# Two fused transformer blocks on one core: the input comes back for the residual tile by tile, into other memory, and the rotary angles are computed later

## The reference

```python
h = rms_norm(x, norm_mix_g[l])
p = h @ w_in[l]
...                      # 8 heads: a chunkwise mLSTM (y_a) and stick-breaking attention (y_b)
y = gates[..., :D_MODEL] * y_a + gates[..., D_MODEL:] * y_b
x = x + y.astype(x.dtype) @ w_out[l]
h2 = rms_norm(x, norm_mlp_g[l])
x = x + jnp.square(jax.nn.relu(h2 @ w_up[l])) @ w_down[l]
```

## Time and profile before

| what | us |
|---|---|
| median of three runs | 1381.68 |
| the profiled execution, its own time | 1377.67 |
| span of that execution, first to last instruction | 1375.9 |
| PE busy | 1319.2 |
| DVE busy | 701.8 |
| ACT busy | 635.1 |
| POOL busy | 101.5 |

### The profile page before, as it was taken

How to read it: one execution, slowest core, us unless ns; L and a number is a source line. 1 busy time by engine, 2 the same in 40 slices (tenths; PEclk the granted TensorE clock), 3 DMA queues, 4 the chain that set the end, 5 groups by cost and what they waited for, 6 DMA issues and landing times.

```text
span 1375.9 us, 16463 instructions
## 1 busy us (share of the span) xinstructions
PE 1319.2 (96%) x5984; PEld 1057.5 (77%) x5984; DVE 701.8 (51%) x1176; ACT 635.1 (46%) x926; POOL 101.5 (7%) x215
## 2 busy tenths in 40 slices
PE   6999999999999997999999999999868999999999
PEld 5787877878777786788888888878656777777887
DVE  5445444544444453542443524453698888435671
ACT  5645455563556552431322313354725545545830
POOL 1000010100001010000000000000121111111000
PEclk9999999999999999999999999999987999999999
DMA  5322212122221224132222322243111233533611
GB/s 200 104 69 96 69 65 84 57 95 69 95 69 65 99 60 158 51 114 81 91 91 95 102 108 91 91 134 116 62 61 39 100 122 104 185 116 130 244 62 61
DMA packets 26531, 134.42 MB, mean 98 GB/s; under 512 B 3320, under 2 KB 4408, under 8 KB 13696
## 3 DMA queue, kind: packets, MB, share of 16 engines
q1 hardware_dynamic: 16992, 107.49, 22.4%
q0 software_dynamic: 4896, 17.03, 3.8%
q10 hardware_dynamic: 4608, 9.44, 1.8%
HBM read 121.35 MB, written 11.55 MB: 97 GB/s over the span
## 4 chain that ended last, share of the span: by engine, by line
PE 89%; DVE 5%; ACT 3%; DMA 2%; issue 1%; POOL 0%; DVEq 0%; ACTq 0%; POOLq 0%
PE proj L291 71%; PE pa L1331 2%; PE pm L1288 1%; DMA x_res<-in_x 1%; PE pm L1338 1%; PE pa L1295 1%; PE pm L1451 1%; PE pa L1451 1%; PE pa L1288 1%; PE pa L1433 1%; PE pm L1433 1%; PE pa L1308 1%; PE pm L1443 1%; DVE rope L1048 1%; PE pm L1317 1%
## 5 line engine op out<-in xcount | busy, mean ns | idle before, releaser
L291 PE MATMUL proj<-h_hi,w_hi 128*128 128x512 f32 x960 | 385.6, 402 | 2.6 <-ACT sq_q L551 1.7
L291 PE MATMUL proj<-h_hi,w_lo 128*128 128x512 f32 x960 | 375.0, 391 | 0.0
L291 PE MATMUL proj<-h_lo,w_hi 128*128 128x512 f32 x960 | 374.7, 390 | 0.0
L264 DVE TENSOR_TENSOR w_lo<-w_raw,w_hi 128x2048 fp32r<-128x2048 f32 x100 | 228.0, 2292 | 151.9 <-ACT w_hi L258 149.7
L258 ACT ACTIVATE w_hi<-w_raw 128x2048 fp32r<-128x2048 f32 x100 | 189.8, 1911 | 147.0 <-PE proj L291 140.2
L291 PEld LDWEIGHTS proj<-h_hi,w_hi 128*128 128x128 f32 x960 | 181.0, 189 | 45.0 <-issue 7.0
L291 PEld LDWEIGHTS proj<-h_hi,w_lo 128*128 128x128 f32 x960 | 180.7, 188 | 38.7
L291 PEld LDWEIGHTS proj<-h_lo,w_hi 128*128 128x128 f32 x960 | 180.9, 188 | 38.4 <-issue 2.9
L291 PE MATMUL proj<-w_hi,act_hi 128*128 128x512 f32 x256 | 99.6, 389 | 0.0
L291 PE MATMUL proj<-w_hi,act_lo 128*128 128x512 f32 x256 | 99.6, 389 | 0.0
L291 PE MATMUL proj<-w_lo,act_hi 128*128 128x512 f32 x256 | 99.6, 389 | 0.0
(11 more groups left out here) (362 smaller groups left out, 1866.2 us busy)
## 6 DMA issues: line engine op xcount, KB each, us to landing
w_raw<-in_wall SPq DMA_DIRECT2D x100, 1024.0 KB, 5.1
gates<-gate_st ACTq DMA_DIRECT2D x24, 256.0 KB, 2.0
m_all<-gates POOLq DMA_DIRECT2D x2, 1536.0 KB, 8.3
x_res<-in_x ACTq DMA_DIRECT2D x4, 512.0 KB, 6.3
bc<-gate_rows POOLq DMA_DIRECT2D x8, 256.0 KB, 3.4
x_res<-in_x POOLq DMA_DIRECT2D x1, 2048.0 KB, 12.8
x<-x_res POOLq DMA_DIRECT2D x1, 2048.0 KB, 7.2
g_all<-gates POOLq DMA_DIRECT2D x1, 2048.0 KB, 14.4
```

Source lines behind the costliest of these rows:

```text
L264: nc.vector.tensor_tensor(w_lo[:, slot, 4 * half:4 * half + 4, :], w_raw[:, half], w_hi[:, slot, 4 * half:4 * half + 4, :], ALU.subtract)\
L291: mm = nc.tensor.matmul(proj[:, bank, :], lhsT, rhs, start=(k == 0 and q == 0), stop=(k == kts - 1 and q == 2))
```

## The change

Three things are changed. `x_res` moves to 32 to 48 KiB of the slab, and `xs`, `relu`, `relu_sq`, the gate rows and the tables of the angles move to make room. The second load of x becomes four DMAs of 512 KB, still from POOL: tiles 0 and 1 once the suffix sums of the last head are made, tiles 2 and 3 once its products with the values are made, each ahead of the loads of the positions and frequencies. On DVE and ACT the code is written in another order: each group's second `split_lo` follows the first addition, the angles follow the third addition of G_OUT, and the two `Sin` follow both groups' `split_hi`.

```diff
--- before.py
+++ after.py
@@ -143,15 +143,15 @@
 
         tok = sb("tok", [P, 4, TB])
         floor = sb("floor", [P, TB])
-        x_res = at("x_res", 61 * K, [P, TB, DM])
-        xs = at("xs", 44 * K, [P, TB, DM])
+        x_res = at("x_res", 32 * K, [P, TB, DM])
+        xs = at("xs", 48 * K, [P, TB, DM])
         act_hi = at("act_hi", 0, [P, KT, SEQ], F32R)
         act_lo = at("act_lo", 16 * K, [P, KT, SEQ], F32R)
-        relu = at("relu", 32 * K, [P, 2, SEQ])
-        relu_sq = at("relu_sq", 36 * K, [P, 2, SEQ])
+        relu = at("relu", 64 * K, [P, 2, SEQ])
+        relu_sq = at("relu_sq", 68 * K, [P, 2, SEQ])
 
         (g_i, g_f, g_abs, g_ls, g_F, g_a, g_G, g_m, one_row) = [
-            at(f"gate_row{i}", (16 + 2 * i) * K, [HEADS, SEQ]) for i in range(9)]
+            at(f"gate_row{i}", (12 + 2 * i) * K, [HEADS, SEQ]) for i in range(9)]
         g_out = at("g_out", 40 * K, [HEADS, 2, SEQ])
         wg_raw = at("wg_raw", 0, [P, KT, P])
         wg_hi = at("wg_hi", 4 * K, [P, KT, P], F32R)
@@ -162,10 +162,10 @@
         w_idx = sb("w_idx", [P, TB, HEADS])
         top8 = sb("top8", [P, 3, 8])
         tick = sb("tick", [P, 33])
-        (ang, turns, angles_c) = [at(f"angles{i}", (40 + i) * K, [P, TB, N_FREQ]) for i in range(3)]
-        pos_i = at("pos_i", 43 * K, [P, TB], mybir.dt.int32)
-        pos_f = at("pos_f", 43 * K + 32, [P, TB])
-        freqs = at("freqs", 43 * K + 64, [P, N_FREQ])
+        (ang, turns, angles_c) = [at(f"angles{i}", (72 + i) * K, [P, TB, N_FREQ]) for i in range(3)]
+        pos_i = at("pos_i", 75 * K, [P, TB], mybir.dt.int32)
+        pos_f = at("pos_f", 75 * K + 32, [P, TB])
+        freqs = at("freqs", 75 * K + 64, [P, N_FREQ])
         q_a2 = at("q_a2", 0, [P, TB, HEADS * QK_M])
         k_a2 = at("k_a2", 12 * K, [P, TB, HEADS * QK_M])
         v_a2 = at("v_a2", 24 * K, [P, TB, HEADS * D_D])
@@ -421,12 +421,16 @@
                     d = z[:, TRI[i]:TRI[i] + P]
                     gp.affine_select(out=d, in_=d, compare_op=ALU.is_gt, fill=NEG, base=0,
                                      pattern=[[1, P]], channel_multiplier=-1).then_inc(S["arg_b_masked"], 1)
+            x_tiles = x_in.rearrange("(t p) d -> p t d", p=P)
+            gp.wait_ge(S["c_made"], HEADS)
+            for t in (0, 1):
+                gp.dma_start(x_res[:, t], x_tiles[:, t]).then_inc(S[f"x_again{t}"], 16)
+            gp.wait_ge(S["pv_b_made"], HEADS)
+            for t in (2, 3):
+                gp.dma_start(x_res[:, t], x_tiles[:, t]).then_inc(S["x_again2"], 16)
             gp.wait_ge(S["head_done"], HEADS + 1)
             for dst, src in ((pos_i, positions), (freqs, inv_freq.broadcast_to([P, N_FREQ]))):
                 gp.dma_start(dst[:], src).then_inc(S["par_landed"], 16)
-            gp.wait_ge(S["x_area_free"], 1)
-            gp.dma_start(x_res[:, :, :], x_in.rearrange("(t p) d -> p t d", p=P)).then_inc(S["x_landed"], 16)
-
 
             gp.wait_ge(S["tile_free"], T_END1)
             gp.dma_start(x2_d.rearrange("(t p) d -> p t d", p=P), x_res[:, :, :]).then_inc(S["x2_stored"], 16)
@@ -610,11 +614,10 @@
             for g in range(G_OUT, G_MLP):
                 for hf in (0, 1):
                     split_hi(g + 1, (g + 1) % 2, hf)
-                if g == G_OUT:
-                    a.wait_ge(S["angles"], len(ANGLES))
-                    a.activation(sine[:, :, :], A3, ACT.Sin).then_inc(S["rope_tables"], 1)
-                    a.activation(cosine[:, :, :], C3, ACT.Sin).then_inc(S["rope_tables"], 1)
-                    a.preload_act_table_set("natural_log_exp_and_others")
+            a.wait_ge(S["angles"], len(ANGLES))
+            a.activation(sine[:, :, :], A3, ACT.Sin)
+            a.activation(cosine[:, :, :], C3, ACT.Sin)
+            a.preload_act_table_set("natural_log_exp_and_others")
             for t in range(TB):
                 a.wait_ge(S["tile_free"], T_MLP - TB + t + 1)
                 norm_rstd(1, t)
@@ -966,24 +969,23 @@
                 v.tensor_tensor(y_lo[:, bass.ds(h, 1), :].rearrange("p a n -> p (a n)"), scl[:, :], yh, ALU.subtract)\
                     .then_inc(S["head_done"], 1)
             v.wait_ge(S["head_done"], HEADS + 1)
-            v.memset(eps[:, :], EPS).then_inc(S["x_area_free"], 1)
-
             for g in range(G_OUT, G_MLP):
-                for hf in (0, 1):
-                    split_lo(g + 1, (g + 1) % 2, hf)
-                if g == G_OUT:
-                    v.wait_ge(S["par_landed"], 128)
-                    for i, (dst, op) in enumerate(ANGLES):
-                        if i:
-                            v.wait_ge(S["angles"], i)
-                        op(v).then_inc(S["angles"], 1)
+                split_lo(g + 1, (g + 1) % 2, 0)
                 for t in range(TB):
                     n = T_OUT + 4 * (g - G_OUT) + t
-                    v.wait_ge(S["x_landed"], 16)
+                    v.wait_ge(S[f"x_again{min(t, 2)}"], 16 if t < 2 else 32)
                     v.wait_ge(S["tile_free"], n)
                     v.wait_ge(S["tile_made"], n + 1)
                     xx = x_res[:, t, 512 * (g - G_OUT):512 * (g - G_OUT + 1)]
                     v.tensor_tensor(xx, xx, proj[:, t % 2], ALU.add).then_inc(S["tile_free"], 1)
+                    if t == 0:
+                        split_lo(g + 1, (g + 1) % 2, 1)
+                    if g == G_OUT and t == 2:
+                        v.wait_ge(S["par_landed"], 128)
+                        for i, (dst, op) in enumerate(ANGLES):
+                            if i:
+                                v.wait_ge(S["angles"], i)
+                            op(v).then_inc(S["angles"], 1)
                     if g == G_MLP - 1:
                         norm_scale(1, t)
             for k in range(KT):
```

## The result

The changed kernel takes 1369.40 us (median of four runs, 1368.28 to 1371.11) against 1381.68 before. The ratio is 0.9913 (95% interval 0.9898 to 0.9929), 12.3 us faster.

A forecast was written before the change was run, and what follows sets the result against it. The prediction took PE to bound the kernel, with a pause ended by the load of x. Removing 7.17 + 1.44 = 8.61 us, with other terms 0, gave 1381.68 - 8.61 = 1373.07 us, range 1370.4 to 1375.9.

The forecast's parts named there:

- What bounds it: Output projection: PE's 7.0 us wait for the addition into x_res is ended by the 2 MB load of x.
- Does the pause go altogether: Output projection: yes; tile 0's bank is free at 513.1, 4.7 us ahead of need, and later tiles are in time.
- A (x late): Output projection: x is late for a tile, a shorter pause stays, 1376 to 1380 us; chance 0.05.
- C (the loads disturb the last head): Last head: loads of x beside its chain hold up work and make the kernel slower, 1386.8 us; chance 0.02.
- D (no effect): Output projection: something other than x holds the first addition, so time stays at 1381.7 us; chance 0.03.
- One sign of being wrong: Last head: the prediction would be wrong if it ended later than 510.0.
- The 2.5 us of delay: Last head: POOL's DMA issue waits while VectorE runs y_hi, making x some 2.5 us later, inside the margins.
- New places: Angles, Sin and statistics in their new order cost 0: angles keep 1.7 us margin, statistics start 0.7 us late.
- The term that is removed: Output projection: the 7.17 us pause plus 1.44 us of slower matmuls behind it go, 8.61 us in all.
- I cannot place these 4.0 us in any row and carry them over whole: Whole kernel: the median's 4.0 us above the profiled execution was kept in the changed kernel's forecast.
- Rival B: Second block: the clock may give part of the gain back or more, up to 2.9 us, 1370.2 to 1376.0; chance 0.26.

The follow-up runs named there:

- e5: The kernel before, run again without edit for a second profile: 1379.57 us against 1380.93, ratio 0.9993.
- e13: The kernel before, no edit, to compare its load of x with its time on one chip: 1381.53 us, ratio 1.0003.
- e16: The kernel before, no edit, to profile an execution from the slower half: 1381.69 us, ratio 0.9999.
- e1: The changed kernel again, no edit: 1369.19 us against 1378.80 for the kernel before, ratio 0.9934.
- e9: The changed kernel on a further chip, no edit: 1369.03 us against 1381.31 for the kernel before, ratio 0.9919.
- e15: The changed kernel on another further chip, no edit: 1369.15 us against 1380.34 for the kernel before, ratio 0.9921.
- e2: The changed kernel with one 2 MB load of x behind the last head and the positions, instead of early loads: 1378.38 us against 1378.80 before.
- e4: The changed kernel with early loads, but both weight splits and the angles ahead of the additions and the two Sin where they were: 1370.37 us.
- e3: The changed kernel with all four loads of x issued only after the last head, ahead of the positions: 1369.27 us, ratio to before 0.9935.
- e10: The changed kernel with five extra VectorE subtractions ahead of the first addition, making a pause without a transfer: 1378.65 us, ratio to before 0.9984.
- e8: The changed kernel with 36 filler matmuls in the second block's 10 us pause and three in each of four short gaps: 1374.81 us.
- e17: The changed kernel with only the 36 filler matmuls in the second block's 10 us pause: 1369.04 us, ratio to before 0.9909.
- e7: The changed kernel with five extra VectorE subtractions ahead of the first addition, on another chip than e10: 1378.74 us, ratio to before 0.9981.
- e6: The kernel before with 28 filler matmuls in the projection's pause, between tiles 1 and 2: 1377.71 us, ratio 0.9982.
- e11: The changed kernel with five extra subtractions and 28 filler matmuls in the pause they make: 1376.59 us, ratio to before 0.9968.
- e12: The changed kernel with three extra subtractions instead of five ahead of the first addition, for a shorter pause: 1373.39 us, ratio to before 0.9945.
- e14: The kernel before with the first group's two weight splits moved behind the first and second additions: 1375.32 us, ratio 0.9963.

## Why the prediction was right in place and too small in size

Executions side by side (the pause is the step between two starts less 0.23; "restart" is the time of the 144 matmuls less the 32.95 of the filled pause; "second block" is from the last addition of the MLP to the end):

| execution | its time | load of x | pause | 144 matmuls | restart | second block |
|---|---|---|---|---|---|---|
| before, first profile | 1377.67 | 12.83 | 7.2 | 34.27 | 1.3 | 462.7 |
| before, e5 | 1379.28 | 13.67 | 8.0 | 34.38 | 1.4 | 462.8 |
| before, e13 | 1379.83 | 13.63 | 8.0 | 34.54 | 1.6 | 462.9 |
| before, e16 | 1382.33 | 13.57 | 7.9 | 35.83 | 2.9 | 464.2 |
| changed, first profile | 1371.11 | early | none | | | 464.2 |
| changed, e1 | 1369.71 | early | none | | | 462.3 |
| changed, e9 | 1368.80 | early | none | | | 461.5 |
| changed, e15 | 1369.15 | early | none | | | 462.2 |

**What bounds it: right.** The chain named the load of x, and e2 gives a pause back by making the load late and whole, with everything else of the change in place.

**Does the pause go altogether: right.** Tile 0's addition ran at 513.26 against a forecast of 512.4, at the head end of that execution 0.5 us later, and no wait is left. Rivals A (x late), C (the loads disturb the last head) and D (no effect) fell: the last `y_hi` came at 508.6 to 510.2 in the profiles without an early load and at 508.6 to 510.3 in those with one. One sign of being wrong did come up, a last head that ends later than 510.0: it ended at 510.58 (509.89 + 0.69). But in the kernel before it ended at 510.65 in e5 and 510.99 in e13, so the limit was set too tight and tells nothing of the loads. The 2.5 us of delay worked out under rival C for a load beside `y_hi` do not follow: a load held up while `y_hi` runs would lose that operation's 0.43 us. The profile did not test it, since POOL had issued its second pair by 509.0 and `y_hi` started at 509.34.

**New places: right.** The margins of the angles and of the statistics came out within 0.2 us. The stage is 42.0 us in every profile of the changed kernel. e4 puts the new order at 0.3 us, and e3 shows that the early issue isn't needed either: it is enough that the load is divided and stands ahead of the positions, the two together.

**The term that is removed: right for the execution, too small for the kernel.** "7.17 + 1.44 = 8.61" is the 8.6 by which the stage shrank between the two first profiles. But the profile of before was of the shortest of its kind: in three further ones the load took 13.6 us and the pause 8.0, 0.8 more, and the restart was once 1.6 us more. The restart varies with the number of slow steps behind the pause: 7 in the first profile, 12 in e2, 14 in e10 and in e16. The Trainium skill, "TensorE: Matmul & The Clock Gate" (section "What's actually happening"), says this of the start of a kernel: the same kernel measures 6, 11 or 14 slow matmuls. Behind a pause, the traces here show as wide a spread. The prediction's sum took the one value that it had read, 1.44 us, and its range allowed twice that; e16 and e10 show 2.9.

**The step that failed** is "I cannot place these 4.0 us in any row and carry them over whole". It treats the distance between the profiled execution and the median as something that both kernels share. They don't share it: the changed kernel's median is 1369.4, against 1369.06 for the sum at the profiled execution. With nothing carried over the time would have been met to 0.3 us. So at least 3.7 of the 4.0 us did not belong to the changed kernel. The runs place them in part. The pause of the kernel before usually lasts 0.8 us longer than in its first profile, since the load does. The artificial pause of 7.1 us costs 9.6 by the medians of e10 and e9, and filled 7.6, so the restart is worth 2.1 us by these medians and not 1.44, another 0.6. By these runs the removed term is 8.6 + 0.8 + 0.6 = 10.0 us and not 8.61.

A gain of 10.0 us is a ratio of 0.9928, and that lies in the interval of each of the four measurements; 0.9938, for 8.6 us, lies only in that of e1. The differences of the medians are 9.6, 11.2, 12.3 and 12.3. What they hold beyond 10.0, up to 2.3 us, is not settled, and medians of the unchanged kernel on one chip differ by up to 1.4. e16 shows where more can lie. It took 4.7 us more than the first profile of before: 2.3 in the projection, 0.9 up to the last `y_hi` (509.7 against 508.8) and 1.5 in the second block, which took 1.4 us longer than in e5. The first changed profile took 1.9 more there than e1. Of the 16 timed runs of before beside e9, ten are above 1380.5 us, at a mean clock of 0.980 to 0.983, and the other six at 0.983 or 0.984, while the changed kernel has one run 3 us or more above its median in each of e9 and e15 (1372.23, 1372.69). Why a kernel without the pause should have such executions more rarely was not shown.

**Rival B** (the clock, either way by up to 2.9 us, 0.26) named the clock, and 0.6 us of what was missing is the clock's, but behind the pause and not in the second block, where B had it. The load's 0.8 us are no part of it. B was centred on zero, while the first profile was already at its cheap end, and the measured 1369.4 lies 0.8 us below even B's 1370.2.

## What to carry to other kernels

- A profiled execution that is faster than every timed run is a warning about its stalls. Read the stall's length and its restart as the low end, and profile the kernel a second time before the difference is added to a forecast for a kernel in which the stall is gone. Here 1.4 of the 4.0 us were found in the stall.
- A transfer that ends a wait is worth dividing so that its first piece serves the first consumer, with the pieces ahead of small transfers on the same queue, before memory is rearranged to issue it earlier. In e3 the two together did it, with the last byte no earlier than before.
- Fillers can keep the clock up, and are a good way to measure what a restart costs. As a remedy they have to lie in a gap that stays: on the chain they cost more than they give (e8), and in the second block they gave nothing even in a gap (e17).

## What was not expected of the hardware

- The same pause of 7.1 us was followed by 34.76 and by 35.83 us for the same 144 matmuls (e7, e10), against 32.95 to 32.99 when it was filled (e6, e11).
- A pause of 2.45 us (e12) left no slow matmul behind it in the profiled execution (32.95 us for the 144); pauses of 3.7 us (e14) and 5.3 us (e2) did.
- A 2 MB load of x took 9.4 us with no weight load beside it (e14), 10.9 with one of 1 MB (e2) and 12.8 to 13.7 with two. Divided into four and issued beside the two weight loads it took as long, 12.8 us from the first issue to the last landing, but its first piece landed after 3.5 (e3).
